# Weights read back with a step: two, four or eight input tiles alternate column by column in each stored group

## The reference, cut to what matters

```python
def swiglu(u, w_gate, w_up, w_down):
    return (jax.nn.silu(u @ w_gate) * (u @ w_up)) @ w_down
```

## Time and profile before

| | |
|---|---|
| median of three runs | 3443.15 us (3440.49 to 3453.31) |
| time of the profiled execution | 3446.24 us |
| its span, first to last instruction | 3444.5 us |
| mean granted TensorE clock | 0.993 |
| PE busy | 3401.3 us, 99% of the span |
| weight loads (PEld) busy | 2744.8 us, 80% |
| DVE busy | 1751.6 us, 51% |
| ACT busy | 1197.3 us, 35% |
| POOL busy | 262.0 us, 8% |
| mean DMA rate | 109 GB/s |

### The profile page before, as it was taken

The page is one execution under the profiler, slowest core; times in us unless marked ns, Lnnn a source line. Parts: engine busy times, 40 slices in busy tenths (PEclk is TensorE's granted clock), DMA queues, the critical chain, the costliest instruction groups (busy, mean ns, idle before and its releaser), DMA issues.

```text
span 3444.5 us, 40836 instructions
## 1 busy us (share of the span) xinstructions
PE 3401.3 (99%) x16686; PEld 2744.8 (80%) x16686; DVE 1751.6 (51%) x3014; ACT 1197.3 (35%) x2021; POOL 262.0 (8%) x219
## 2 busy tenths in 40 slices
PE   8999999999999999999999999999999999999999
PEld 7888886778888888887777888888778777878887
DVE  7666446565665733334655643334553555354433
ACT  3222336543222332223555332224322444233322
POOL 0000210002000200021100100013011000020000
PEclk9999999999999999999999999999999999999999
DMA  7565322123565533223210322323221223122332
GB/s 254 201 213 193 109 84 71 41 71 112 190 230 196 184 102 101 98 92 113 75 44 31 110 86 86 110 81 102 72 81 65 68 76 124 40 96 90 97 107 80
DMA packets 120361, 376.36 MB, mean 109 GB/s; under 512 B 13296, under 2 KB 28272, under 8 KB 120176
## 3 DMA queue, kind: packets, MB, share of 16 engines
q1 hardware_dynamic: 120176, 373.76, 32.9%
HBM read 371.61 MB, written 2.10 MB: 108 GB/s over the span
## 4 chain that ended last, share of the span: by engine, by line
PE 93%; DVE 4%; ACT 2%; issue 0%; DMA 0%; POOL 0%; SPq 0%; DVEq 0%; ACTq 0%; POOLq 0%
PE ps L451 26%; PE ps L453 26%; PE ps L452 26%; PE ps L673 2%; PE ps L696 2%; PE ps L568 2%; PE ps L485 1%; PE ps L486 1%; PE ps L487 1%; PE ps L501 1%; PE ps L494 1%; DVE s_wl L1492 1%; ACT s_wh L971 0%; PE ps L540 0%; PE ps L539 0%
## 5 line engine op out<-in xcount | busy, mean ns | idle before, releaser
L1492 DVE TENSOR_TENSOR s_wl<-s_raw,s_wh 128x1024 fp32r<-128x1024 f32 (+3 forms) x645 | 704.2, 1093 | 894.3 <-ACT s_wh L971 893.3
L451 PE MATMUL ps<-s_uh,s_wh 128*128 128x512 f32 x2824 | 1128.0, 399 | 10.0 <-DVE s_ul L1553 3.8
L453 PE MATMUL ps<-s_ul,s_wh 128*128 128x512 f32 x2824 | 1104.1, 391 | 0.4 <-issue 0.4
L452 PE MATMUL ps<-s_uh,s_wl 128*128 128x512 f32 x2824 | 1103.1, 391 | 0.0
L971 ACT ACTIVATE s_wh<-s_raw 128x1024 fp32r<-128x1024 f32 (+3 forms) x645 | 588.1, 914 | 706.9 <-PE ps L453 499.7
L451 PEld LDWEIGHTS ps<-s_uh,s_wh 128*128 128x128 f32 x2824 | 532.5, 189 | 152.7 <-issue 40.1
L453 PEld LDWEIGHTS ps<-s_ul,s_wh 128*128 128x128 f32 x2824 | 531.9, 188 | 113.7 <-issue 0.8
L452 PEld LDWEIGHTS ps<-s_uh,s_wl 128*128 128x128 f32 x2824 | 532.6, 189 | 107.6 <-issue 2.4
L451 PE MATMUL ps<-s_fh,s_wh 128*128 128x512 f32 x960 | 373.6, 389 | 0.2 <-DVE s_wl L1492 0.2
L452 PE MATMUL ps<-s_fh,s_wl 128*128 128x512 f32 x960 | 373.5, 389 | 0.0
L453 PE MATMUL ps<-s_fl,s_wh 128*128 128x512 f32 x960 | 373.5, 389 | 0.0
(11 more groups left out here) (419 smaller groups left out, 3344.3 us busy)
## 6 DMA issues: line engine op xcount, KB each, us to landing
s_raw<-w SPq DMA_DIRECT2D x616, 512.0 KB, 3.6
s_raw<-w SPq DMA_DIRECT2D x96, 192.0 KB, 2.4
s_raw<-w SPq DMA_DIRECT2D x64, 256.0 KB, 2.6
s_raw<-w SPq DMA_DIRECT2D x19, 128.0 KB, 2.1
s_x<-x SPq DMA_DIRECT2D x4, 512.0 KB, 6.5
out<-s_x SPq DMA_DIRECT2D x8, 256.0 KB, 2.2
s_raw<-w SPq DMA_DIRECT2D x4, 420.0 KB, 4.2
s_crow<-crow SPq DMA_DIRECT2D x2, 512.0 KB, 5.9
```

Of the source, the lines that this page charges most:

```text
L451: TE.matmul(o, w_hi(i, k), h, start=first, stop=False)
L452: TE.matmul(o, w_lo(i, k), h, start=False, stop=False)
L453: return TE.matmul(o, w_hi(i, k), l, start=False, stop=last)
L1492: V.tensor_tensor(wl[w][:, 0:n], raw[t % NRAW][:, 0:n], wh[w][:, 0:n].bitcast(F32), SUB).then_inc(*s_lo.up(("lo", t)))
```

## The change

The host stores each split piece of width 128 in another order. Its nk input tiles are taken in sets of s, and within a set the columns alternate: column 0 of tile 0, column 0 of tile 1, and so on to tile s - 1, then column 1 of each. s is 2, 4 or 8, by the piece's slot, halved until it divides nk; pieces of three input tiles, and those of other widths, keep s = 1. On the chip `w_hi` and `w_lo` return the same numbers as before by a slice with step s, that is one element every 8, 16 or 32 bytes. No instruction is added or taken away, and no wait.

```diff
+STRIDES = (2, 4, 8)
...
+def strides(todo):
+    out, n = {}, 0
+    for i, (name, _, nk, _, w, parts) in enumerate(todo):
+        s = STRIDES[n % NW]
+        while nk % s:
+            s //= 2
+        out[i] = s if w == 128 else 1
+        n += parts
+    return out
...
+    stride = strides(todo)
+
+    def cut(t, i, k):
+        w, s = todo[i][4], stride[i]
+        a = k // s * s * w + k % s
+        return t[slot[i]][:, a:a + (w - 1) * s + 1:s]
+
     def w_hi(i, k):
-        w = todo[i][4]
-        return wh[slot[i]][:, k * w:(k + 1) * w]
+        return cut(wh, i, k)
 
     def w_lo(i, k):
-        w = todo[i][4]
-        return wl[slot[i]][:, k * w:(k + 1) * w]
+        return cut(wl, i, k)
...
-    for name, k0, nk, c0, w, _ in todo:
-        n = 128 * nk * w
-        stream[o:o + n].reshape(128, nk, w)[:] = M[name][128 * k0:128 * (k0 + nk), c0:c0 + w].reshape(nk, 128, w).transpose(1, 0, 2)
+    for i, (name, k0, nk, c0, w, _) in enumerate(todo):
+        n, s = 128 * nk * w, stride[i]
+        stream[o:o + n].reshape(128, nk // s, w, s)[:] = M[name][128 * k0:128 * (k0 + nk), c0:c0 + w].reshape(nk // s, s, 128, w).transpose(2, 0, 3, 1)
         o += n
```

## The result

The changed kernel takes 3573.36 us in the median (3566.02 to 3575.5), against 3443.15 before: the ratio is 1.0358 with a 95% interval of 1.0335 to 1.038. The profiled execution took 3566.02 us, 119.8 more than the one before. Its span, from the first instruction to the last, is 3564.2 us, against 3444.5. The page first; the shares and the chain answer to the earlier trace rows, the two groups to the earlier trace rows. The lines have moved: 451 to 453 are now 470 to 472, 568 is 587, 673 is 692.

The account below looks back on a forecast made before the run. TensorE, through the distances between matmuls, was taken to bound the kernel. 0 us in the steady stream plus 15.5 us for exposed first loads on 3443.15 gave 3458.7, rounded to 3459, with a range of 3415 to 3600.

Parts of the forecast that it names:

- The likeliest case: Whole kernel: loads hidden in the stream, extra time only at 218 places; 15.5 us more, 3459 us.
- the outgrown load: Feed of whole pieces: the stepped load takes longer than the 227 ns distance; at 237 ns 99 us more, 3558; chance 0.17.
- the forecast: Whole kernel: hidden in the stream, exposed at 218 places; 3459 us, own range 3448 to 3468, chance 0.37.
- The sign that was named for being wrong: Between matmul starts: the prediction is wrong if any steady distance has changed by more than 1 ns.
- What bounds the kernel: TensorE, busy in 99% of the span: a nanosecond added to a matmul's distance from its neighbour is added to the end.
- What moves: DMAs, roundings, subtractions and moving operands stay the same; only the step with which weight loads read changes.
- The steady stream: Matmuls inside pieces: loads of 216 ns fit under 227, with 11 ns left; 0 us.
- the loose bound of 268: Source line 591's pace: at most 2.1 ns a column, 268 ns for 128 columns; 336 us as upper end.
- The exposed loads: First loads behind a small matmul or a wait: 145 of 218 grow by 107 ns, 15.5 us.
- Loads take read slots: Beside the moving stream: each 16-byte block read costs it a cycle; 357 us more, 3816; chance 0.14.
- the step costs nothing: Weight loads: the array takes one column per clock wherever it lies; 3443 us, chance 0.20.
- clears the way: In the stream: a jumping load meets the moving stream less often; 36 us less, 3407, or all, 3305; chance 0.12.

Follow-up runs that it names:

- matmuls alone: Kernel of nothing but matmuls, 32 in a row of each kind, without the reference's computation; at 512 columns 227, 233, 235, 244 ns for s = 1, 2, 4, 8.
- the gates alone: Against the changed kernel, only the gate projections' pieces (gA, gB, zg) keep their steps, all others contiguous: 3476.36 us against 3448.5 for the kernel before, ratio 1.0073.

## Why the prediction was wrong

The likeliest case was 15.5 us more; 130 us came. That 3573 lies inside the range of 3415 to 3600 is due to the room left for a rival, the outgrown load, and not to the forecast, whose own range ended at 3468. The sign that was named for being wrong, a distance in the stream changed by more than 1 ns, is there at every step.

**What bounds the kernel** was right: the nanoseconds added to the distances appear one for one in the span.

**What moves** was right in its terms: no other engine or queue took longer, and waits changed by a few microseconds only.

**The steady stream is the step that failed**: "213 + 3 = 216 ns are under 227 ... 0 us". It came to 118 us, in two parts.

The larger is the size of the load. The stepped row of the trace before gave 1.74 ns a column, and for its own step of 64 bytes that is right: such loads run at 222 ns where they set the pace, 1.74 a column. I carried it to steps of 16 and 32 bytes, for which the trace had no row, and rounded it down to twice the contiguous time. Those steps cost 233 and 241 ns. Against the 226.7 of matmuls alone that is 6.6 ns on 4,068 and 14.6 on 3,576 matmuls: 27 + 52 = 79 us. Both 213 and 223 were under the cover and gave 0; the loose bound of 268 gave 336 us; the truth lay between, a few per cent over a cover with 11 ns of margin, where every nanosecond costs 7.6 us.

The smaller part, 39 us, is that a load under its cover isn't free beside a stream of fp32r matmuls with 512 columns: 6.0 ns at s = 2, which the trace of before gave no row for (23 us), and the rest over the load's own pace at s = 4 and 8 (1.4 and 2.8 ns, 6 and 10 us). For contiguous loads the experiments show such a cost to depend on how far load and moving operand lie apart, down to 4 bytes; with s = 2 no start removed it; and with plain float32 (s = 4, 8, 16) and bf16 (s = 2 to 32) it is absent. The 118 us are those of the table; the traces put matmul against matmul give 114. The rule quoted from the Trainium skill ("SBUF — State Buffer", "Door 1: The DMA port swizzle") holds for the load by itself: with step 2 the matmul takes the contiguous 120 ns at N 256 (at N 64, where loads set the pace, 118 ns against 112), with steps 4 and 8 not. For the kernel it misleads, since step 2 everywhere costs 65 us. The other rule of the Trainium skill ("TensorE: Matmul & The Clock Gate", "Step-by-step: what each phase is for"), that a load takes no read bandwidth from a running matmul, agrees here with plain float32 (429 ns at s = 1, 4, 8 and 16) and not with fp32r: 227 became 233 with a load that had time to spare.

**The exposed loads** were right: 15.5 us predicted, 15.8 in the trace, and shown apart by the gates alone. The fit is in part luck: the growth was 115 and 124 ns a load, not 107, on 133 loads, not 145, and the two errors cancel.

**The rivals.** "The load outgrows its cover" is what happened at s = 4 and 8. It was priced at 99 us and those two steps took 95, by luck: 8 and 17 ns, not 13 each. It left out s = 2. "Loads take read slots" foresaw that s = 2 would pay, and had size and reason wrong: 13 and 40 ns by the number of blocks, where 6, 8 and 17 were measured and fewer loaded columns don't help. What disturbs the stream is not settled: that the relative placement of contiguous operands matters, and that multiples of 256 bytes do no harm, is shown; by which mechanism isn't. Nor is the source of the 13.4 ns that stay at the best placement; bf16, at 216 ns, has only 2.5 of them. That the step costs nothing, or clears the way, is refuted for loads of 128 columns beside 512, at every step tried.

## What to carry to other kernels

A cost read from one row holds for that row's shape; where the cover has a margin of a few per cent and stands behind thousands of instructions, price the range and not the middle, for it is the margin that is being forecast. Beside fp32r matmuls of 512 columns keep stationary operands contiguous, and start both operands of a matmul at the same offset modulo 256 bytes, at a multiple of 32 bytes. A load that is hidden by its duration can still slow the work that hides it: compare distances between starts, not busy times.

## What the hardware showed that I had not expected

- Stepped loads of 128 four-byte columns don't get steadily slower. Beside 256 moving columns the distance is 120 ns at s = 2, 233 at s = 4, 241 at s = 8 and 222 at s = 16; beside 512 it is 268 ns at s = 12 and 240 at s = 32.
- Weights that lie contiguous, but 16 bytes further on, cost a kernel of 3450 us 57 us.
- Of the three formats tried beside 512 moving columns only fp32r was disturbed by stepped loads: plain float32 took 429 ns at s = 1, 4, 8 and 16, bf16 216 ns at s = 1 to 32.
- A stepped moving operand is dearer still: with contiguous weights, 512 columns took 453, 461 and 431 ns at steps of 2, 4 and 8 elements, twice the contiguous 227.
